# Expert weights in slabs of 2 MB: 16 KB of a partition in one run, a ring of eight places

## The reference, cut to what matters

```python
def expert_choice_ffn(h, w_router, w_gate, w_up, w_down):   # 16 experts, D = 1024, F = 2048
    cap = EC_CAPACITY * S // N_EXPERTS                      # 64 tokens for each expert
    aff = softmax(einsum('bsd,de->bse', h, w_router))
    gates, idx = lax.top_k(aff.transpose(0, 2, 1), cap)
    xe = h[bidx, idx]
    a = einsum('becd,edf->becf', xe, w_gate)                # w_gate: 16 x 1024 x 2048
    b = einsum('becd,edf->becf', xe, w_up)                  # w_up:   16 x 1024 x 2048
    ye = einsum('becf,efd->becd', silu(a) * b, w_down)      # w_down: 16 x 2048 x 1024
    return zeros_like(h).at[bidx, idx].add(ye * gates[..., None])
```

## Time and profile before

| | |
|---|---|
| time, median of 3 runs | 2095.17 us |
| the profiled execution: its own time / its span | 2097.64 / 2095.8 us |
| TensorE busy | 1948.5 us (93%) |
| DMA share and rate, 320 to 1180 us | 1.01, 422 GB/s |
| experts, first product to copy of the last result | 272.4 to 1206.4 us |

### The profile page before, as it was taken

The page is one execution under the profiler, slowest core; times in us unless marked ns, Lnnn a source line. Parts: engine busy times, 40 slices in busy tenths (PEclk is TensorE's granted clock), DMA queues, the critical chain, the costliest instruction groups (busy, mean ns, idle before and its releaser), DMA issues.

```text
span 2095.8 us, 23298 instructions
## 1 busy us (share of the span) xinstructions
PE 1948.5 (93%) x9049; PEld 1139.0 (54%) x9049; DVE 845.4 (40%) x1273; ACT 572.8 (27%) x901; POOL 37.3 (2%) x40
## 2 busy tenths in 40 slices
PE   7989899999999999999999987999999999999898
PEld 6656633322222222222222266888888788778786
DVE  6874621111111111111110166456466576876443
ACT  4453410000000000000000044443133433357651
POOL 1023000000000000000000000000000000000000
PEclk9998999999999999999999999999999999999999
DMA  8422399999999999999999953445345232211101
GB/s 258 161 93 73 156 361 421 422 421 422 422 422 422 422 421 422 422 422 422 422 422 422 420 184 118 167 161 192 114 143 181 81 94 87 81 61 41 41 21 41
DMA packets 132179, 528.11 MB, mean 252 GB/s; under 512 B 10006, under 2 KB 55892, under 8 KB 82836
## 3 DMA queue, kind: packets, MB, share of 16 engines
q1 hardware_dynamic: 129492, 520.56, 63.0%
q0 software_dynamic: 1008, 3.52, 0.7%
q10 hardware_dynamic: 1616, 3.15, 0.4%
HBM read 524.97 MB, written 2.23 MB: 252 GB/s over the span
## 4 chain that ended last, share of the span: by engine, by line
PE 53%; DMA 35%; DVE 6%; ACT 3%; issue 1%; SPq 1%; ACTq 0%; DVEq 0%
DMA w_expert<-in_w_up 17%; DMA w_expert<-in_w_gate 16%; PE bank L1085 6%; PE bank L889 5%; PE bank L890 5%; PE bank L891 5%; PE bank L868 5%; PE bank L869 5%; PE bank L870 5%; PE bank L908 1%; PE bank L1095 1%; DMA raw<-in_w_ple_gate 1%; SPq L714 1%; PE bank L1303 1%; DVE full L1772 1%
## 5 line engine op out<-in xcount | busy, mean ns | idle before, releaser
L1085 PE MATMUL bank<-w_expert,chosen 128*64 128x512 f32 x2048 | 483.7, 602 | 62.0 <-DMA w_expert<-in_w_up 45.7
L1085 PEld LDWEIGHTS bank<-w_expert,chosen 128*64 128x64 f32 x2048 | 130.4, 136 | 395.4 <-issue 232.9
L1954 DVE TENSOR_TENSOR x_res<-x_res,bank 128x512 f32<-128x512 f32 x136 | 87.3, 684 | 428.4 <-PE bank L1104 408.1
L1095 PE MATMUL bank<-w_expert,hidden_t 128*64 128x512 f32 x1024 | 229.9, 596 | 5.9 <-ACT hidden_t L1515 4.6
L1709 DVE TENSOR_TENSOR w_lo<-raw,w_hi 128x2048 fp32r<-128x2048 f32 x75 | 171.9, 2292 | 156.5 <-ACT w_hi L1350 156.5
L1350 ACT CAST w_hi<-raw 128x2048 fp32r<-128x2048 f32 x75 | 142.8, 1904 | 152.9 <-PE bank L891 136.4
L868 PE MATMUL bank<-act_hi,w_hi 128*128 128x512 f32 x424 | 173.4, 409 | 0.1
L1976 DVE TENSOR_TENSOR hidden_rows<-gate_silu,bank 128x512 f32<-128x512 f32 x32 | 20.6, 684 | 364.1 <-PE bank L1085 364.1
L870 PE MATMUL bank<-act_hi,w_lo 128*128 128x512 f32 x424 | 166.1, 392 | 0.0
L869 PE MATMUL bank<-act_lo,w_hi 128*128 128x512 f32 x424 | 166.0, 391 | 0.0
L1095 PEld LDWEIGHTS bank<-w_expert,hidden_t 128*64 128x64 f32 x1024 | 74.6, 137 | 138.7 <-issue 121.1
(11 more groups left out here) (287 smaller groups left out, 2484.7 us busy)
## 6 DMA issues: line engine op xcount, KB each, us to landing
w_expert<-in_w_gate SPq DMA_DIRECT2D x128, 1024.0 KB, 24.9
w_expert<-in_w_up SPq DMA_DIRECT2D x128, 1024.0 KB, 26.5
w_expert<-in_w_down SPq DMA_DIRECT2D x128, 1024.0 KB, 26.5
raw<-in_a_w_in SPq DMA_DIRECT2D x24, 1024.0 KB, 6.3
raw<-in_b_w_in SPq DMA_DIRECT2D x16, 1024.0 KB, 5.2
raw<-in_a_ada_w SPq DMA_DIRECT2D x12, 1024.0 KB, 5.3
raw<-in_b_ada_w SPq DMA_DIRECT2D x12, 1024.0 KB, 6.3
raw<-in_kv_ada_w SPq DMA_DIRECT2D x8, 1024.0 KB, 5.8
```

Of the source, the lines that this page charges most:

```text
L1085: last = mm(PS[b0 + n][HALF[x], :], XE[:, k % 4, HALF[k // 4]], WE[place][:, r], start=(k == 0), stop=(k == KD - 1), skip_group_check=True)
L1095: last = mm(PS[4][HALF[x], :], HT[:, 2 * q + k, HALF[half]], WE[place][:, r], start=(i == 0 and k == 0), stop=(i == 7 and k == 1), skip_gr ...
L1954: tt(part, part, ps[:, :], ALU.add).then_inc(d_add, 1)
```

## The change

The expert slabs become twice as large: 2 MB, of which a partition gets 16 KB in one run. For gate and up these are two neighbouring rows (row s x 256 + 2p + k), for down four. The contraction runs over the same rows in another grouping, so the transposes that lay out the chosen tokens and the hidden values read every second and every fourth column (`turn_chosen`, `turn_hidden`). An expert has 12 slabs, the ring has eight places of 16 KB (128 KB of a partition, before 96 KB). Small tiles move out of the way, the hidden values (`HR`) now lie where the silu of the gate (`GSIL`) does. Since 12 slabs do not go evenly into 8 places, the loops of SP and TensorE run over pairs of experts. TensorE signals a used slab after every second step, and waits for a load before every second step. The places lie in another order, and their first loads wait for other events. The row of norm_ple_post gets a tile of its own (`GROW_E`), loaded behind the slabs of w_ple_gate.

```diff
@@ -19,8 +19,9 @@
-SLABS_E = 24
-RING_E = 12
+SLAB_E = 2 * SLAB
+SLABS_E = 12
+RING_E = 8
@@ -107,8 +108,9 @@
-        E_PLACES = (24, 32, 40, 56, 72, 112, 120, 16, 48, 64, 172, 180)
-        WE = [at(f"w_expert{i}", kb, [P, SLAB]) for i, kb in enumerate(E_PLACES)]
+        E_PLACES = (172, 32, 112, 16, 48, 64, 96, 140)
+        WE = [at(f"w_expert{i}", kb, [P, SLAB_E]) for i, kb in enumerate(E_PLACES)]
...
@@ -692,57 +695,57 @@
-            sp.wait_ge(filled, fill_no(("pool", 3)))
+            sp.wait_ge(filled, fill_no(("ot1", 3)))
             sp.dma_start(PTOK[:, :, :], a["p"][0, 0].rearrange("(t p) d -> p t d", p=P)).then_inc(s_p, 16)
-            sp.dma_start(GROW[:, :], bc(a["norm_ffn"], 0, D)).then_inc(s_grow, 16)
             sp.dma_start(CL[:, :], c_late).then_inc(s_late, 16)
             sp.dma_start(QGS, c_steep).then_inc(s_late, 16)
+
+            wg, wu = (a[x][0].rearrange("e (s p k) f -> e s p (k f)", p=P, k=2) for x in ("w_gate", "w_up"))
+            wd = a["w_down"][0].rearrange("e (s p k) d -> e s p (k d)", p=P, k=4)
+
+            def load_expert(e, i, place):
+
+                src = (wg, wu)[i // 4][e, i % 4] if i < 8 else wd[e, down_slab(i - 8)]
...
             for g in range(RING_E):
-                if g < 3:
-                    _, kind, i = stream[N_E - 4 + g]
+                if g == 1:
+                    for n in (N_E - 3, N_E - 2):
+                        _, kind, i = stream[n]
+                        sp.wait_ge(lo_ready, i + 1) if kind == "W" else sp.wait_ge(ada_fold, fold_done(i))
+                if g == 2:
+                    sp.wait_ge(filled, fill_no(("wout", 1, 3)))
+                if g == 3:
+                    _, kind, i = stream[N_E - 4]
                     sp.wait_ge(lo_ready, i + 1) if kind == "W" else sp.wait_ge(ada_fold, fold_done(i))
-                if g == 3:
-                    sp.wait_ge(filled, fill_no(("wout", 1, 3)))
+                    sp.wait_ge(lo_ready, W_PROJ + 1)
+                if g == 4:
+                    sp.wait_ge(filled, fill_no(("proj", 1, 3)))
                 if g == 7:
-                    sp.wait_ge(lo_ready, W_PROJ + 1)
-                if g == 8:
-                    sp.wait_ge(filled, fill_no(("proj", 1, 3)))
-                if g == 11:
-                    sp.wait_ge(k_step, 5 + 16 + 3)
+                    sp.wait_ge(filled, fill_no(("pos_t",)))
                 load_expert(0, g, g)
-            with sp.Fori(0, NE - 1) as e:
-                for q in range(SLABS_E):
-                    sp.wait_ge(e_used, e * SLABS_E + (q + 1))
+            with sp.Fori(0, NE // 2 - 1) as e:
+                for q in range(2 * SLABS_E):
...
-            sp.wait_ge(n_xn, 8)
-            sp.dma_start(GROW[:, :], bc(a["norm_ple_post"], 0, D)).then_inc(s_grow, 16)
             for n in range(N_E, len(stream)):
                 _, kind, i = stream[n]
                 if n < N_E + RING:
-                    sp.wait_ge(e_used, e_last(16 + 8 * slot(n)))
+                    sp.wait_ge(e_used, e_last(16 + 16 * (slot(n) // 2)))
+                if n == N_E + RING:
+                    sp.wait_ge(e_used, e_last(140))
+                    sp.dma_start(GROW_E[:, :], bc(a["norm_ple_post"], 0, D)).then_inc(s_grow, 16)
...
@@ -1062,7 +1065,8 @@
-                    last = nc.tensor.transpose(PS[6][:, c * P:(c + 1) * P], XG[:, c * P:(c + 1) * P], ident)
+                    cols = XG[:, c // 2 * 256:(c // 2 + 1) * 256].rearrange("p (j k) -> p k j", k=2)[:, c % 2, :]
+                    last = nc.tensor.transpose(PS[6][:, c * P:(c + 1) * P], cols, ident)
...
@@ -1081,20 +1084,22 @@
-                        r = slice(x * D + n * 512, x * D + (n + 1) * 512)
-                        last = mm(PS[b0 + n][HALF[x], :], XE[:, k % 4, HALF[k // 4]], WE[place][:, r],
+                        c0 = k % 2 * F + x * D + n * 512
+                        last = mm(PS[b0 + n][HALF[x], :], XE[:, k % 4, HALF[k // 4]], WE[place][:, c0:c0 + 512],
                                   start=(k == 0), stop=(k == KD - 1), skip_group_check=True)
-                last.then_inc(e_used, 1)
+                if k % 2:
+                    last.then_inc(e_used, 1)
...
@@ -1112,35 +1117,37 @@
-            with pe.Fori(0, NE) as e:
-                for n in range(SLABS_E):
-                    place = n % RING_E
+            with pe.Fori(0, NE // 2) as pair:
+
+                for m in range(4 * SLABS_E):
+                    n, place, e, e_add = m % (2 * SLABS_E), m // 2 % RING_E, pair * 2, m // (2 * SLABS_E)
                     if n == 0:
-                        pe.wait_ge(v_xe, e + 1)
-                    pe.wait_ge(e_loaded[place], e * (16 * SLABS_E // RING_E) + 16 * (n // RING_E + 1))
+                        pe.wait_ge(v_xe, e + (e_add + 1))
+                    if n % 2 == 0:
+                        pe.wait_ge(e_loaded[place], pair * (16 * 2 * SLABS_E // RING_E) + 16 * (m // 2 // RING_E + 1))
                     if n < 16:
...
```

More of the change, by code:

```diff
@@ L702, in _ @@
             load(N_E - 1)
-            wg, wu = (a[x][0].rearrange("e (k p) f -> e p k f", p=P) for x in ("w_gate", "w_up"))
-            wd = a["w_down"][0].rearrange("e (q p k) d -> e q p k d", p=P, k=2)
-            def load_expert(e, i, place):
-                if i < 16:
-                    src = (wg, wu)[i // 8][e, :, i % 8:i % 8 + 1, :]
-                else:
-                    src = wd[e, down_slab(i - 16)]
-                sp.dma_start(WE[place][:, :].rearrange("p (k n) -> p k n", k=1 if i < 16 else 2), src
-                             ).then_inc(e_loaded[place], 16)
@@ L735, in _ @@
                         sp.sem_inc(place_free, 1)
[L736 to L737 removed]
+                    load_expert(e * 2 + r // SLABS_E, r % SLABS_E, r % RING_E)
+            for g in range(RING_E + (NE - 2) * SLABS_E, NE * SLABS_E):
                 sp.wait_ge(e_used, g - RING_E + 1)
                 load_expert(g // SLABS_E, g % SLABS_E, g % RING_E)
[L740 removed]
@@ L1074, in turn_hidden @@
                 for j in range(4):
-                    q, k = 2 * half + j // 2, j % 2
-                    cols = HR[:, q * 256:(q + 1) * 256].rearrange("p (c k) -> p k c", k=2)[:, k, :]
+                    cols = HR[:, half * 512:(half + 1) * 512].rearrange("p (c k) -> p k c", k=4)[:, j, :]
                     last = nc.tensor.transpose(PS[half][:, j * P:(j + 1) * P], cols, ident)
@@ L1083, in expert_in @@
                     for x in range(2):
-                        r = slice(x * D + n * 512, x * D + (n + 1) * 512)
-                        last = mm(PS[b0 + n][HALF[x], :], XE[:, k % 4, HALF[k // 4]], WE[place][:, r],
+                        c0 = k % 2 * F + x * D + n * 512
+                        last = mm(PS[b0 + n][HALF[x], :], XE[:, k % 4, HALF[k // 4]], WE[place][:, c0:c0 + 512],
                                   start=(k == 0), stop=(k == KD - 1), skip_group_check=True)
-                last.then_inc(e_used, 1)
+                if k % 2:
+                    last.then_inc(e_used, 1)
             def expert_out(place, i):
-                q, half = i // 2, i % 2
-                for k in range(2):
+                q, half = i // 4, i // 2 % 2
+                for k in (2 * (i % 2), 2 * (i % 2) + 1):
                     for x in range(2):
-                        r = slice(k * D + x * 512, k * D + (x + 1) * 512)
-                        last = mm(PS[4][HALF[x], :], HT[:, 2 * q + k, HALF[half]], WE[place][:, r],
-                                  start=(i == 0 and k == 0), stop=(i == 7 and k == 1), skip_group_check=True)
-                last.then_inc(e_used, 1)
+                        c0 = k * D + x * 512
+                        last = mm(PS[4][HALF[x], :], HT[:, 4 * q + k, HALF[half]], WE[place][:, c0:c0 + 512],
+                                  start=(i == 0 and k == 0), stop=(i == 7 and k == 3), skip_group_check=True)
+                if i % 2:
+                    last.then_inc(e_used, 1)
             def combine(t, base_):
@@ L1991, in _ @@
             for t in range(NT):
-                stt(out=E_[:, t, :], in0=E_[:, t, :], scalar=ERSTD[:, t:t + 1], in1=GROW[:, :],
+                stt(out=E_[:, t, :], in0=E_[:, t, :], scalar=ERSTD[:, t:t + 1], in1=GROW_E[:, :],
                     op0=ALU.mult, op1=ALU.mult).then_inc(k_step, 1)
```

65 lines of the change are left out of this document (34 added, 31 removed).

## The result

The changed kernel takes 2079.7 us (median of 4 runs, 2079.6 to 2081.1) against 2095.4 us before (also four runs): a ratio of 0.9919, 95% interval 0.9905 to 0.9933. I had forecast 2072.2 us with a range of 2062 to 2088.5. So it is faster and in the range, but the gain is two thirds of the one I worked out. Two later sets of runs, each beside the kernel before, gave 0.9907 (0.9891 to 0.9923) and 0.9904 (0.9888 to 0.9921).

A forecast was written before the change was run, and what follows sets the result against it. Loads were taken to bound the expert stage. Deeper ring -8.6, faster rate -16.0 and longer tail +1.7 gave -22.9, rounded to -23 us, subtracted from the 2095.17 us median: 2072.2 us, range 2062 to 2088.5.

The forecast's parts named there:

- What bounds the kernel: Expert stage: the loads set its end, needing 59.7 us an expert against 52.8 us for TensorE.
- The landing's start: Wait for w_ple_proj ahead of the expert loads: the next load's issue stays at 258.85 us, its data counting from 261.05.
- Term 1: Start of the expert loads, 272 to 297 us: a deeper ring keeps the queue full and gains 8.6 us.
- Term 2: Expert loads' rate: 16 KB packets bring a 2 MB slab from 4.971 to 4.886 us, 16.0 us gained over 188.
- Term 3: Tail behind the last expert landing: 16 instead of 8 MATMUL are left, 1.7 us lost.
- The rest: Everything after the copy of the last expert result: untouched, 890 us.
- Cut rows: Rival on expert loads: a 16 KB run goes out as two 8 KB packets, 8.8 us gained, 2086.4 us; chance 0.12.
- A cap at 425 GB/s: Rival on expert loads: something other than packets holds the rate, 425.5 GB/s, 15 us gained, 2080.2 us; chance 0.14.
- Large rows slow: Rival on expert loads: 16 KB runs lose more than packets save, 2179 us or, at full price, above 3100; chance 0.04.
- Clock: Rival in the expert stage: longer TensorE waits lower its clock, 40 us slower, 2135 us; chance 0.04.
- No dip under 420 GB/s after 262 us: Sign for Term 1 at the start of the expert loads: the DMA rate never falls below 420 GB/s after 262 us.
- The waits enter the chain: Sign in the expert stage: TensorE's first waits for a load enter the chain near 500 us instead of 406.

The follow-up runs named there:

- split_tail: Changed kernel with the very last expert slab loaded as two DMAs of 1 MB, TensorE waiting for the second only before its last eight products: 2075.1 us, ratio 0.9896.
- second and third execution: The changed kernel profiled again, unchanged, in two later sets of runs: 2079.0 us (ratio 0.9907) and 2075.5 us (ratio 0.9904).
- half_dmas: Changed kernel with each slab loaded by two DMAs of 1 MB, partitions 0 to 63 and 64 to 127: 2992 us, ratio 1.4268.

## Why the prediction was right, and where it was off

**What bounds the kernel: right.** The loads set the end, and both the rate and the start's dip moved it. Taking back the rate alone costs some 14 us of the gain (2093.2), the ring alone some 7 (2085.6).

**The landing's start: right.** The wait for w_ple_proj stands where it stood (258.85 and 257.9 us); load 4 landed 7.2 to 7.6 us behind its issue, where 2.2 + 4.886 = 7.1 us was expected.

**Term 1, 8.6 us: too large by 1.6 to 3.3 us.** Up to slab 24 the kernel before lost 8.9 us against its own rate (115.6 - 7.3 - 20 x 4.970), the changed one 3.6, 1.9 and 3.4 us. So the ring gave back 5.3 to 7.0 us. By the mean of the sixteen events it gave back 6.9 us in each execution (7.9 lost before, 1.0 now); the rest is that the last engine falls behind the others. Two steps failed.

The first is the margin: "Each must be issued 2.2 us before the load ahead of it lands ... all four are in time". Load 10 was issued 3.7 to 3.9 us ahead of the landing in front, and was 0.8 to 1.1 us late in all three executions. The events say why. An engine runs dry when it has done its own share, not when the load has landed: the first one had finished load 9 only 2.1 us behind the issue of load 10, and all sixteen events of load 10 are 0.2 us late or more. Load 9 was issued 3.0 us ahead of the first engine, and more than half of its events are under 0.1 us late; in the kernel with runs of 8 KB load 10 was 2.8 us ahead of the first engine and in time. 2.1 us is at the edge: in `split_tail`, which is the same up to there, load 10 had no more and its middle events are under 0.1 us late. So the 2.2 us, read from the fastest landing, was nearly right, but it counts from the first engine that is done, and at load 9 the engines were 1.6 to 1.9 us apart. Why the last events of load 10 shift by 0.8 to 1.1 us, more than the 0.3 to 0.4 of the middle ones, stays open.

The second is a term that the sum put at nothing, the kernel's own instructions, which are moved by DMA too. From 280 to 345 us the changed kernel's trace has, beside the loads' queue:

```profile
q8 instruction: 3, 0.05, 0.3%
q14 instruction: 1, 0.01, 0.0%
```

From 260 to 370 us there are six such packets, of 8 KB (266.2 and 297.9 us) and 16 KB (283.9, 313.2, 340.0 and 366.2 us; each took 1.0 to 1.1 us). Each falls into one load, 5, 9, 11, 14, 19 and 25, and there one event moves back against the steady rate, by some 0.9 us for the small packets and 1.4 to 1.7 us for the large ones; apart from loads 9 and 11 the other fifteen stay. The second and third execution show the same, with loads 8 and 20 in place of 9 and 19. From load 26 on no packet comes and no event moves by 0.5 us. An engine that has fallen behind stays behind, so the landing is late only by what the last engine loses: 0.3 to 0.6 us at load 5, 0.9 and 1.0 us at load 8 (second and third execution), 1.6 and 1.0 us at load 14 (first and third). In the second, one engine lost 1.6 us at load 14 as well, but it was one of the first and the landing doesn't show it. That is luck, and nearly all of the difference between the 1.9 and the 3.4 to 3.6 us. The trace doesn't name the engine of a packet; that the packets are the cause is read from their falling together, six of six in three executions.

**Term 2, 16.0 us: 14.1.** The mechanism was right, the packet's price too high. Two full stretches, and the same view of the changed kernel, give 49819c + 362.79r = 13760 and 25296c + 368.34r = 13760: c = 8.3 ns, r = 36.8 us a MB. My second equation was a stretch of 8 us with packets of 2 KB and 128 engine-us to divide, and gave 9.5 ns. A slab has 144 packets fewer: 144 x 8.3 / 16 = 0.075 us instead of 0.085, and x 188 = 14.1. The changed slab takes 4.895, not 4.886 us.

**Term 3, +1.7 us: +1.8.** The copy comes 3.8 us behind the last landing instead of 2.0, and 23.4 us behind the last up slab (1164.4 to 1187.8), where 23.2 was predicted for either path. The two split kernels show that both paths count: splitting the down slab alone gave nothing, both 1.5 us (the up slab alone wasn't tried).

**The rest: right within noise.** 890.0 us behind the copy against 889.4.

**The sum.** From the issue to the copy: -5.3 to -7.0, -14.1, +1.8, gives -17.6 to -19.3; measured -17.6, -19.0 and -17.9. Predicted was -22.9. The experts' end moved by 18.6 and the span by 18.0 us. That leaves 2.5 of the 7.5 us between 2072.2 and 2079.7: the profiled execution of before was 2.5 us above its median and the one of after at its own, so a difference of medians is 15.5 where that of the two executions is 18.0. I had named that distance and then subtracted from the median; the same kernel's medians in three sets are 2075.5 to 2079.7.

**Rivals.** Cut rows: out, packets are of 16384 B (its time, 2086.4, is missed too). A cap at 425 GB/s: its time, 2080.2, is the nearest of all, and by accident; the rate is 428 in every full stretch, so the time is the sum of other shortfalls. The Trainium skill's 425 GB/s (HBM Reference, "Specifications (TRN2)") is exceeded by 3 GB/s for 860 us here. Large rows slow: out for slabs of 128 partitions, 615 ns a packet. Its evidence, the 198 GB/s of the earlier trace rows, has another reading: these were two loads of 64 neighbouring partitions each, one behind the other (lines 774 to 777), with 1246 ns a packet, and `half_dmas` has 1221 ns for the same pattern on SP's queue. I had looked at the length of the rows and not at their partitions. Clock: out for this change, the wait of 1.24 us in front of each slab of gate and up leaves it at 1.00; with 4.38 us it fell to a mean of 0.80.

**Signs.** "No dip under 420 GB/s after 262 us" failed, at 412 for 290 to 300 us, and that was the sign of the failed margin. The waits enter the chain at 430 us, not near 500: slab 24 landed at 366.5 us and TensorE wanted it at 271.5 + 24 x 4.40 = 377.1, a lead of 10.6 us that shrinks by 0.495 a slab, so it is gone near slab 45 (the first one in the chain landed at 429.86 + 29.67 = 459.5 us and is slab 43). The depth of the ring, by which I had argued, doesn't enter once the stream is unbroken.

## What to carry to other kernels

Once a stage is bound by loads, its end is an issue, the lost time at its start, and a count times a rate: measure the three apart, by landings. Longer contiguous runs lower the price of the packets (by the fit 8.3 ns each, 1.5% from 8 to 16 KB), and how many DMAs carry them hardly counts. What a deeper ring gains is only the time in which the queue would have been nearly empty, and for that a refill must be issued a latency ahead of the first engine that is done, not of the landing (2.1 us was mostly too late here, 2.8 us in time; ahead of the landing these were 3.7 to 4.2 and 4.7 us). A load moved ahead of a wait gave 1.0 us more, an earlier start of the consumer 1.6 us; a further place was not tried. Where single executions differ by a microsecond or two, compare the mean of a load's events before its landing: the landing shows the one engine with the worst luck.

## What the runs showed of the hardware that was not expected

- Two DMAs of 64 neighbouring partitions each, one behind the other in one queue, moved 215 GB/s; the same bytes by even and odd partitions 428 GB/s. Packets of 16 KB took 1221 instead of 615 ns, and the DMA share read 1.01 in both, so a full share doesn't mean full speed.
- With a ring of eight slabs of 256 packets, SP's issue of one load took 2.6 to 6.5 us from 430 us on, 4.5 in the median; with eight of 128 packets 0.33 us. It cost nothing: a slab took 4.969 us, as before.
- Ahead of the gather TensorE stood still for 3.3 and 1.4 us, and the gather took 6.3 us for its 16 MATMUL at a granted clock of 0.56; with products in the first gap it took 3.65 us at 1.00.
- A packet of the instruction queue (16 KB, 1.0 to 1.1 us) set one of sixteen event series of the loads back by 1.4 to 1.7 us, and it didn't catch up while the queue was full: at load 14 the landing was 1.6 us later for it in one execution, and no later in another.
